# Two attention stages of a two-block model on one core: copies ahead of exponentials, masks added on VectorE, a gate projection two steps sooner

## The reference

```python
logits = einsum('bhqd,bhkd->bhqk', qb, k) * scale + fq[..., :, None] - F[..., None, :]
logits = where(kpos[None, :] <= qpos[:, None], logits, -inf)
p = softmax(logits, axis=-1)
out = einsum('bhqk,bhkd->bhqd', p, v)
```

## Time and profile before

| | |
|---|---|
| median of three runs | 2177.53 us (2177.52 to 2177.66) |
| the profiled execution | 2177.74 us |
| its span | 2176.0 us |
| TensorE busy | 2135.4 us, 98% of the span |
| weight loads busy | 1730.3 us, 80% |
| VectorE busy | 1285.1 us, 59% |
| ScalarE busy | 917.7 us, 42% |
| granted TensorE clock, mean | 0.995 of full speed |
| read from HBM | 188.09 MB, 88 GB/s over the span |

### The profile page before, as it was taken

The page is one execution under the profiler, slowest core; times in us unless marked ns, Lnnn a source line. Parts: engine busy times, 40 slices in busy tenths (PEclk is TensorE's granted clock), DMA queues, the critical chain, the costliest instruction groups (busy, mean ns, idle before and its releaser), DMA issues.

```text
span 2176.0 us, 26697 instructions
## 1 busy us (share of the span) xinstructions
PE 2135.4 (98%) x10620; PEld 1730.3 (80%) x10620; DVE 1285.1 (59%) x1966; ACT 917.7 (42%) x1550; POOL 101.5 (5%) x155
## 2 busy tenths in 40 slices
PE   9999999999999999999999999999999999999998
PEld 7866688888888658888888878777788878888887
DVE  6446475555347767655543749456677657555634
ACT  4235553334325456333432642344445545333421
POOL 0000040000000003100000000000012200000000
PEclk9999999999999999999999999999999999999999
DMA  5312123333323203333332323202222023333332
GB/s 201 97 59 78 60 96 97 97 97 116 97 78 107 68 30 126 97 97 97 116 97 88 126 78 90 75 30 87 79 77 68 2 78 98 97 97 98 117 97 77
DMA packets 51099, 194.00 MB, mean 89 GB/s; under 512 B 5665, under 2 KB 5665, under 8 KB 49953
## 3 DMA queue, kind: packets, MB, share of 16 engines
q1 hardware_dynamic: 50976, 192.30, 28.1%
HBM read 188.09 MB, written 4.19 MB: 88 GB/s over the span
## 4 chain that ended last, share of the span: by engine, by line
PE 88%; DVE 5%; ACT 5%; issue 1%; DMA 1%; SPq 0%; ACTq 0%; DVEq 0%
PE bank L403 26%; PE bank L404 26%; PE bank L405 26%; PE bank L980 2%; PE bank L703 1%; DMA ring<-stream 1%; ACT arena L1265 1%; PE bank L681 1%; DVE small L1889 1%; ACT whi L1160 1%; PE bank L618 1%; DVE arena L2010 0%; DVE xs L1884 0%; PE bank L692 0%; PE bank L775 0%
## 5 line engine op out<-in xcount | busy, mean ns | idle before, releaser
L403 PE MATMUL bank<-xs,whi 128*128 128x512 f32 (+2 forms) x1992 | 770.8, 387 | 8.4 <-DVE xs L1884 2.9
L405 PE MATMUL bank<-xs,wlo 128*128 128x512 f32 (+2 forms) x1992 | 750.1, 377 | 0.0
L404 PE MATMUL bank<-xs,whi 128*128 128x512 f32 (+2 forms) x1992 | 749.9, 376 | 0.0
L1863 DVE TENSOR_TENSOR wlo<-ring,whi 128x1024 fp32r<-128x1024 f32 x333 | 415.2, 1248 | 294.8 <-ACT whi L1160 294.3
L1160 ACT ACTIVATE whi<-ring 128x1024 fp32r<-128x1024 f32 x333 | 350.4, 1054 | 262.4 <-DMA ring<-stream 262.2
L403 PEld LDWEIGHTS bank<-xs,whi 128*128 128x128 f32 x1992 | 375.4, 188 | 93.4 <-issue 12.2
L405 PEld LDWEIGHTS bank<-xs,wlo 128*128 128x128 f32 x1992 | 375.2, 188 | 69.0
L404 PEld LDWEIGHTS bank<-xs,whi 128*128 128x128 f32 x1992 | 375.8, 189 | 67.2 <-issue 2.9
L403 PE MATMUL bank<-whi,xs 128*128 128x512 f32 (+1 forms) x808 | 314.8, 390 | 1.6 <-issue 0.9
L405 PE MATMUL bank<-whi,xs 128*128 128x512 f32 (+1 forms) x808 | 311.7, 386 | 0.0
L404 PE MATMUL bank<-wlo,xs 128*128 128x512 f32 (+1 forms) x808 | 311.6, 386 | 0.0
(11 more groups left out here) (367 smaller groups left out, 1781.3 us busy)
## 6 DMA issues: line engine op xcount, KB each, us to landing
ring<-stream SPq DMA_DIRECT2D x333, 512.0 KB, 3.6
arena<-gains SPq DMA_DIRECT2D x5, 1024.0 KB, 5.8
arena<-xt SPq DMA_DIRECT2D x4, 512.0 KB, 6.1
arena<-xn SPq DMA_DIRECT2D x1, 2048.0 KB, 8.0
kept<-arena SPq DMA_DIRECT2D x1, 2048.0 KB, 7.2
arena<-kept SPq DMA_DIRECT2D x1, 2048.0 KB, 8.0
out<-arena SPq DMA_DIRECT2D x3, 512.0 KB, 2.6
con<-consts SPq DMA_DIRECT2D x1, 744.0 KB, 11.6
```

What stands on the lines that cost most here:

```text
L403: nc.tensor.matmul(out, ah, bh, start=first, stop=False)
L404: nc.tensor.matmul(out, ah, bl, start=False, stop=False)
L405: return nc.tensor.matmul(out, al, bh, start=False, stop=last)
L1863: V.tensor_tensor(wlo[:, v % SLOTS, :], ring[:, v % SLOTS, :], whi[:, v % SLOTS, :], ALU.subtract).then_inc(wlo_done, 1)
```

## The change

- In both attentions ScalarE's transposed copy stands ahead of the step's exponential, in the forgetting attention the result copy too.
- The sparse attention's 32 masks leave TensorE. VectorE's maximum becomes one `tensor_tensor_reduce`: logits plus mask, times -1, written back to the logits' bank, with the minimum as result. The exponential takes `scale=-1.0`. The wait for the masks moves from TensorE to VectorE.
- In the sparse attention the transposes stand three steps behind the logits and the values four; the loops have one step more. The three early splits move from steps 1, 9, 17 to 5, 13, 21.
- The `mo` pieces begin in step 0, and the output projection's first parts and operand splits come some two steps sooner.
- `den` of the last mLSTM head goes to bank 5 and its `ms` to bank 6.
- Weight unit 1 is requested ahead of the parameters.

```diff
             for q in range(4):
                 sp.dma_start(U[:, 2 * q:2 * q + 2, :], xt[:, 2 * q:2 * q + 2, :]).then_inc(x_sem[q], 16)
+            sp.dma_start(ring[:, 1, :], stream[1]).then_inc(ring_sem[1], 16)
             sp.dma_start(par[:], params).then_inc(par_sem, 16)
-            for s in (1, 2, 3):
+            for s in (2, 3):
...
+        def den_bank(h):
+            return 7 if h < ML_HEADS - 1 else 5
+
+        def square_bank(h):
+            return 7 if h < ML_HEADS - 1 else 6
...
-        MO_FIRST, MO_STEP = 2, 7
+        MO_FIRST, MO_STEP = 0, 7
...
-        operand_at = {30: (0,), 31: (1,), 32: (2, 4), 33: (5, 3), 34: (6,)}
+        operand_at = {28: (0,), 29: (1,), 30: (2,), 31: (4,), 32: (3,), 33: (5,), 34: (6,)}
...
         dsa_steps = [dict(w=(i + 1) * P, q=dq[:, h, i * P:(i + 1) * P], k=dk[:, h // 4, 0:(i + 1) * P],
-                          more=[(idb[:], madd[:, i, 0:(i + 1) * P] if i else mqb[:], 0, (i + 1) * P)],
+                          mask=madd[:, i, 0:(i + 1) * P] if i else mqb[:],
...
             def attention(name, steps, between=None):
...
-                        if n == 1:
-                            pe.wait_ge(vector_out, vector_at.find("masks"))
-                        nc.tensor.matmul(bank[b][:, 0:W], st["q"], st["k"], start=True, stop=False)
-                        for x, (l, r, c0, c1) in enumerate(st["more"]):
-                            m = nc.tensor.matmul(bank[b][:, c0:c1], l, r, start=False, stop=x == len(st["more"]) - 1)
-                        m.then_inc(tensor_out, tensor_at.next(name, "logits", n))
+                        nc.tensor.matmul(bank[b][:, 0:W], st["q"], st["k"], start=True, stop=True).then_inc(tensor_out, tensor_at.next(name, "logits", n))
...
-                    if 2 <= n < N + 2:
-                        k, st = n - 2, steps[n - 2]
+                    if 3 <= n < N + 3:
+                        k, st = n - 3, steps[n - 3]
...
-                    if n >= 3:
-                        k, st = n - 3, steps[n - 3]
+                    if n >= 4:
+                        k, st = n - 4, steps[n - 4]
...
                 if x == 0 and 0 <= h < ML_HEADS:
-                    claim(7)
+                    b = den_bank(h)
+                    claim(b)
                     pe.wait_ge(vector_out, vector_at.find("ml", "summed", h))
...
-                if 32 <= n < 37:
+                if 30 <= n < 35:
                     for half in (0, 1):
-                        out0_part(n - 32, 1, half)
+                        out0_part(n - 30, 1, half)
...
             def attention(name, steps, between=None, ahead=None):
...
+                    if 3 <= n < N + 3:
+                        k, st = n - 3, steps[n - 3]
+                        act.wait_ge(tensor_out, tensor_at.find(name, "t", k))
+                        if k >= 3:
+                            act.wait_ge(tensor_out, tensor_at.find(name, "pv", k - 3))
+                        A(st["ts"][:, 0:st["w"]], bank[5 + k % 2][:, 0:st["w"]], ACT.Copy).then_inc(scalar_out, scalar_at.next(name, "pt", k))
                     if n < N:
...
-                        A(st["ps"][:, 0:W], bank[st["lb"]][:, 0:W], ACT.Exp, bias=small[:, 200 + n % 4:201 + n % 4],
+                        A(st["ps"][:, 0:W], bank[st["lb"]][:, 0:W], ACT.Exp, bias=small[:, 200 + n % 4:201 + n % 4], scale=-1.0,
...
-                    if x == 1 and j < COUNT["z2b"]:
+                    if x == 5 and j < COUNT["z2b"]:
                         split_units(FIRST["z2b"] + j + AHEAD)
...
+                        logits, top = bank[steps[n]["lb"]][:, 0:steps[n]["w"]], small[:, 200 + n % 4:201 + n % 4]
+                        if name == "dsa":
+                            if n == 1:
+                                dve.wait_ge(vector_out, vector_at.find("masks"))
+                            V.tensor_tensor_reduce(logits, logits, steps[n]["mask"], -1.0, 3e38, ALU.add, ALU.min, top).then_inc(vector_out, vector_at.next(name, "max", n))
```

54 lines of the change are left out of this document (25 added, 29 removed).

## The result

| | before | changed |
|---|---|---|
| median of 4 runs each, us | 2177.53 | 2159.26 |
| lowest to highest | 2177.06 to 2177.66 | 2157.74 to 2162.55 |
| the profiled execution, time / span | 2177.74 / 2176.0 | 2157.74 / 2156.0 |
| its mean granted clock | 0.995 | 0.998 |

The ratio is 0.9919, with a 95% interval of 0.9901 to 0.9936.

The account below looks back on a forecast made before the run. TensorE, busy 98% of the span, was taken to bound the kernel. Opening -1.2, forgetting attention -2.8 and sparse attention -7.5 summed to -11.5 us, giving 2166.0 us from the median, range 2162.0 to 2171.0.

Parts of the forecast that it names:

- So clock and bandwidth drop out there: In the two attentions, full granted clock and 10 to 18% of transfer capacity in use; neither was counted as a limit.
- Opening, -1.2: Before `mq`: weight unit 1, requested ahead of the 407.5 KB of parameters, lands sooner and TensorE gains 1.2 us.
- Forgetting attention, -2.8: Sum of bank changes, earlier gate projection, copies ahead and a shorter output wait: -2.8 us, bounds -0.2 and -5.8.
- The start: Start of forgetting attention: banks 5 and 6 remove 2.5 us of waits, `den` waits 0.4 for bank 5; net -2.1.
- the gate projection: Forgetting attention, `mo` two steps sooner: longer waits for the read of bank 7, +1.4 at unit 1, +0.5 at unit 3.
- the copies: Forgetting attention: copies ahead of exponentials remove TensorE's waits, 1.4 us for transposed and 0.7 for result copies; -2.1.
- Sparse attention, -7.5: Masks off TensorE, the first stall and a small late one removed, the new maximum covered: -7.5 us, range -5.5 to -7.5.
- the first stall: Sparse attention, step 1: TensorE's 1.69 us wait for p behind a split goes, -1.7, and 0.2 near the end.
- The masks: Sparse attention: 32 masks off TensorE save 4.3 us by columns, plus 1.3 at the short ones; 5.6 taken.
- New maximum: VectorE in sparse attention: 0.69 us at 512 columns plus 0.1 for a second instruction, covered except 0.5 at the end.
- (a): Rival: forgetting attention gives nothing back because late reads of bank 7 eat its gains; 2168.8 us, chance 0.18.
- (d): Rival: later stages absorb gains as TensorE waits for weights or VectorE, leaving masks' 4.3 us less some; 2174, chance 0.06.

Follow-up runs that it names:

- the order alone: Kernel before with only the sparse attention's deeper loop, copies ahead of exponentials and later splits, masks left on TensorE; 2170.92 us, ratio 0.9964.

## Why the prediction missed

**What bounds the kernel**: right. TensorE is 98% busy before and after, the chain is TensorE's, and each microsecond taken off it moved the end.

**"So clock and bandwidth drop out there"**: right for the attentions in the profiled execution (in others dips came there too, at 180 to 196 us and in the first sparse stall), wrong as a statement on the whole. The sum had no term for the clock elsewhere, and the range no width for it. The rows of the page with tenths of the clock do not show the dips; stretches of 4 us do. It is 4.5 us of the 20.0 between the two profiled executions and about 3 of the 18.3 between the medians (15 at one clock), and the same kernel shows it between its own runs (2171.7 to 2179.6 us before, 59 runs). Without it the three stages alone, -15.5, give 2162.0 us, the lower end of the range: the sparse attention took the time to that edge, and the clock took it over.

**Opening, -1.2**: the mechanism right, the size a little high; 0.9 us on the mean over fourteen executions, beside which the first product's own place scatters by 0.5. The parameters land 1.03 to 1.06 us behind the unit, so their 407.5 KB come at some 390 GB/s and not at the 340 of the whole phase.

**Forgetting attention, -2.8; measured -3.9.** The start and the gate projection together were right in size, -0.7 forecast (-2.1, +1.4, +0.5, -0.5) and about -0.6 measured with the copies out of the way, but not in their parts, and that is luck: the read of bank 7 cost 2.07 and 0.79 us (2.4 and 1.0 walked), while the wait before the output grew from 0.85 to 1.94 us instead of falling to 0.35. I had moved it with everything else; but the products before it came sooner and its operand not by as much. The term that failed is the copies, -2.1 for -3.3: I had counted only waits that the profile names, and with the copies ahead the stage became shorter by 0.8 us more than its printed waits did (3.3 and 2.5). That these are short late starts, as in the sparse attention, was not followed up here. Without the copies the gate's move would have gained nothing, which the sum, adding term by term, did not see.

**Sparse attention, -7.5; measured -10.1.** The step that failed is the first stall, -1.7 and -0.2. I took the printed stalls for all that the order could give, and so put the forecast on the upper end of the stage's own range, 5.5 to 7.5. The order gave 5.7 us: 2.75 in the first head, where 1.7 were printed and some 0.4 are only work (two transposes, one value product) that now stands behind it, 0.95 in each of two later heads with a split (9.07 against 8.12), about 0.3 in three others (8.40), none in the second, 0.2 in the last, which has that work now. These were in the trace, as distances between first logits, 9.07 and 8.40 us in turn. The masks went the other way, -5.6 forecast and -4.4 measured in the new order (65.70 to 61.32); the lower bound, the columns, was the right value. In the old order they were worth 1.9. The two errors cover each other in part, 3.8 us too little for the order and 1.2 too much for the masks: 0.16 us at each short mask was booked as mask and was a late p.

**New maximum, rivals (a) to (d)**: full rate; VectorE was nowhere the bound, though with twice the passes 2.7 us came through. (a) did not occur, since the copies gave more than the reads took; (d) did not occur, the 15.5 us of the three stages all reached the end. None of the three signs that were to show the forecast wrong came up (a slow maximum, copies with new waits, TensorE idle further on): they all looked for too little gain, and it failed by too much.

## What to carry to other kernels

Where an engine is nearly always "busy", measure the period of a repeated step against what its instructions need: alternation between periods (9.07 and 8.40 us here) shows an engine that sets the pace where no wait is printed. Price an operation on such an engine by the periods with and without it, in the order that it will stand in: 4.3 us of masks were worth 1.9 in the one order and 4.4 in the other. Compare kernels at one granted clock before a difference of 0.2% is given to a cause.

## What the runs showed of the hardware that was not expected

- A late operand of a transpose is not printed as a wait when it is short: starts came 0.1 to 0.3 us late while the profile counted TensorE busy for most of it, and with the same instructions its busy time in the sparse attention fell from 69.15 to 65.49 us.
- A mask of 128 columns in bf16 between fp32 products costs 0.06 us, its columns, and the transpose behind it starts without a further gap when its operand is there (seven times in the run with the order alone).
- The maximum with a mask added takes 296, 433, 563 and 696 ns at 128 to 512 columns, in place in PSUM, and 142 ns more for its second instruction.
- The granted clock falls to its lower level for some microseconds behind waits of TensorE of 0.8 to 2.5 us in some executions and not in others with the same instructions around; a dip at 180 us cost 1.0 us, one at 191 us and those outside the attentions about 1.4 each. The Trainium skill (TensorE: Matmul & The Clock Gate, Part 1) says that the gate watches activity on a beat of its own, not the program's, so that one kernel shows it differently from run to run; the scatter here agrees with that. That the waits cause the dips was not tested: no run was made that fills them.
